# Gated delta rule: q's norm folded into the output's norm, with q's squares added on GpSimd

## The reference, cut to what is computed

```python
def l2norm(x):
    return x * rsqrt(sum(x * x, -1) + 1e-6)

q = l2norm(silu(conv(q_raw))) * 128 ** -0.5       # 8 heads of 128, each used by two value heads
k = l2norm(silu(conv(k_raw)))
# per value head (16) and direction (2), chunk by chunk:
#   qk = einsum(q, k) * decay
#   o_i = (q * exp(gc)) @ S + qk @ v_new
o = o_forward + flip(o_backward)
o = o * rsqrt(mean(o * o, -1) + 1e-6) * g_norm     # per token and head
y = (o * silu(z)) @ w_out
```

## Time and profile before

| | |
|---|---|
| median of 3 runs | 3367.14 us |
| lowest and highest | 3359.4 and 3367.23 us |
| span of the profiled execution | 3362.7 us |
| PE busy | 3184.5 us, 95% |
| DVE, ACT, POOL busy | 52%, 44%, 19% |
| granted TensorE clock, mean | 0.978 |

### The profile page before, as it was taken

How to read it: one execution, slowest core, us unless ns; L and a number is a source line. 1 busy time by engine, 2 the same in 40 slices (tenths; PEclk the granted TensorE clock), 3 DMA queues, 4 the chain that set the end, 5 groups by cost and what they waited for, 6 DMA issues and landing times. The chain is left out here.

```text
span 3362.7 us, 57300 instructions
## 1 busy us (share of the span) xinstructions
PE 3184.5 (95%) x22569; PEld 2066.8 (61%) x22569; DVE 1745.8 (52%) x3567; ACT 1475.9 (44%) x3027; POOL 637.6 (19%) x524
## 2 busy tenths in 40 slices
PE   5779999999999999999999999897999999999998
PEld 2347777777777764455445555444676767767663
DVE  1146666666666652244433334244666766666642
ACT  3135545545545531156423445234455555555521
POOL 0013322322232220011001010002323232232300
PEclk9789999999999999999999999897999999999999
DMA  9811111111111127022311012001112111111135
GB/s 376 305 40 39 41 45 34 50 41 45 50 41 45 31 65 261 0 61 67 123 32 38 25 39 88 32 16 50 36 43 55 42 54 38 54 40 42 42 109 193
DMA packets 216679, 238.16 MB, mean 71 GB/s; under 512 B 19290, under 2 KB 159780, under 8 KB 216292
## 3 DMA queue, kind: packets, MB, share of 16 engines
q1 hardware_dynamic: 216420, 234.57, 21.7%
HBM read 214.87 MB, written 19.66 MB: 70 GB/s over the span
## 5 line engine op out<-in xcount | busy, mean ns | idle before, releaser
L917 PE MATMUL ps<-hT,W 128*128 128x512 f32 (+1 forms) x2656 | 1007.9, 507 | 2.9 <-DVEq L192 2.0
L917 PEld LDWEIGHTS ps<-hT,W 128*128 128x128 f32 x2656 | 467.6, 192 | 206.0 <-issue 164.9
L1349 DVE CAST_PREDICATED arena<-mask,ps 128x384 bf16<-128x384 uint32 x448 | 252.5, 564 | 242.1 <-PE ps L986 180.0
L1168 ACT CAST arena<-ps 128x384 bf16<-128x384 f32 x384 | 166.5, 479 | 339.4 <-PE ps L973 339.0
L2352 PE MATMUL ps<-arena 128*128 128x512 f32 x712 | 311.1, 595 | 2.7 <-SPq L192 2.5
L1351 DVE CAST_PREDICATED arena<-mask,ps 128x384 bf16<-128x384 uint32 x448 | 249.9, 558 | 0.0
L2352 PEld LDWEIGHTS ps<-arena 128*128 128x128 f32 x712 | 134.6, 191 | 167.4 <-issue 162.6
L1987 PE MATMUL ps<-hT,W 128*128 128x512 f32 (+1 forms) x608 | 218.2, 493 | 0.9 <-DMA W<-in_att_w_in 0.7
L1461 POOL TENSOR_TENSOR arena<-arena 128x768 f32<-128x768 f32 (+1 forms) x32 | 43.5, 1360 | 921.2 <-ACT arena L1204 921.2
L1324 DVE SCALAR_TENSOR_TENSOR arena<-arena,vec 128x770 f32<-128x770 f32 (+1 forms) x192 | 189.6, 988 | 6.8
L986 PEld LDWEIGHTS ps<-arena 128*128 128x128 bf16 x2304 | 147.1, 99 | 50.8 <-issue 45.7
(11 more groups left out here) (290 smaller groups left out, 6105.9 us busy)
## 6 DMA issues: line engine op xcount, KB each, us to landing
arena<-in_ada_w SPq DMA_DIRECT2D x24, 2048.0 KB, 19.7
W<-in_gdn_w_in SPq DMA_DIRECT2D x95, 512.0 KB, 4.0
W<-decay_rows SPq DMA_DIRECT2D x64, 384.0 KB, 4.9
arena<-in_gdn_w_out SPq DMA_DIRECT2D x32, 512.0 KB, 10.3
W<-in_gdn_w_out SPq DMA_DIRECT2D x30, 512.0 KB, 3.4
arena<-gated SPq DMA_DIRECT2D x32, 384.0 KB, 8.2
gated<-arena SPq DMA_DIRECT2D x24, 384.0 KB, 2.4
W<-in_att_w_in SPq DMA_DIRECT2D x16, 512.0 KB, 4.0
```

The costliest lines, as they stand in the source:

```text
L917: mm = pe.matmul(ps[:, b, 0:t1 - t0], w[:, i, :], env.hT[:, i, t0:t1], start=(i == 0), stop=(i == KD - 1))
L1168: act.copy(half_cols(Xb[d], s, d), ps[:, 2 * d, 0:384].rearrange("p (c b s) -> p c b s", c=NT, s=s)).then_inc(*inxe.up(m, lv, d))
L1349: dve.copy_predicated(half_cols(Mb[d], s, d), wide(env.m4[:, d, lv]), src_m).then_inc(*inm.up(m, lv, d, "m"))
```

## The change

For q the sum by ones, Ln, Exp, the two table loads and DVE's product are taken out; G and the scan use q as SiLU leaves it. POOL forms q · (1e-6 · 128²) and multiplies that by q, into two new buffers `q2` (a q head serves two value heads, and the next q comes before the second is done). At the end of a slot POOL adds `q2` to the squares of o before PE may sum them. G and the decay rows no longer wait for `nrm` of q but for its SiLU. The new buffers move the tiles behind them by 6144 bytes per partition. Since the layer gets two more semaphores, some of the LRU's and the attention's are taken from this layer's names.

```diff
@@ fill_plan
-        normed = (["x1"] if short else ["x0", "x1"]) * (tile and n > -2)
+        normed = ["x0", "x1"] * (tile and n > -2 and n % 2 == 0)
@@ gdn_phase
-    v = carve(env, [..., ("sq", (T,)),
+    v = carve(env, [..., ("sq", (T,)), ("q2", (T,), 2),
...
-    xrs = seq("x_rs", [(n,) for n in TILES])
-    nrm = seq("nrm", [(n,) for n in TILES])
+    xrs = seq("x_rs", [(n,) for n in TILES if n % 2 == 0])
+    nrm = seq("nrm", [(n,) for n in TILES if n % 2 == 0])
...
+    qsc = seq("q_scaled", [(n,) for n in TILES if n % 2])
+    osf = seq("osf", [(m,) for m in U])
@@ tensor, fill
-                    if starts:
+                    if starts and n % 2 == 0:
                         pe.wait_ge(nrm.sem, nrm.at(n))
+                    elif starts:
+                        pe.wait_ge(sx.sem, sx.at(n, 1))
@@ scalar, keep
-                sc, e = (1.0 / P, 0) if use[0] == "o" else (1.0, 0) if n % 2 == 0 else (float(P), 1)
+                sc, e = (1.0 / P, 1) if use[0] == "o" else (1.0, 0)
@@ vector
-                if p == 14 and n in TILES:
-                    t = v.k if n % 2 == 0 else v.q
+                if p == 14 and n in TILES and n % 2 == 0:
                     dve.wait_ge(xrs.sem, xrs.at(n))
-                    lo = q_from(n)
-                    dve.tensor_tensor(t[:, lo:T], t[:, lo:T], v.sq[:, lo:T], ALU.mult).then_inc(*nrm.up(n))
+                    dve.tensor_tensor(v.k, v.k, v.sq, ALU.mult).then_inc(*nrm.up(n))
@@ gpsimd
             if n in TILES:
-                t = v.k if n % 2 == 0 else v.q
                 pool.wait_ge(sx.sem, sx.at(n, 1))
-                pool.wait_ge(og.sem, og.at(n - 1, 0))
                 lo = q_from(n)
-                pool.tensor_tensor(v.sq[:, lo:T], t[:, lo:T], t[:, lo:T], ALU.mult).then_inc(*sqx.up(n))
+                if n % 2 == 0:
+                    pool.wait_ge(og.sem, og.at(n - 1, 0))
+                    pool.tensor_tensor(v.sq, v.k, v.k, ALU.mult).then_inc(*sqx.up(n))
+                else:
+                    q2 = v.q2[(n + 1) // 2 % 2][:, lo:T]
+                    pool.tensor_scalar(q2, v.q[:, lo:T], EPS * P * P, None, ALU.mult).then_inc(*qsc.up(n))
+                    pool.wait_ge(qsc.sem, qsc.at(n))
+                    pool.tensor_tensor(q2, q2, v.q[:, lo:T], ALU.mult).then_inc(*sqx.up(n))
             if m in U:
-                pool.wait_ge(nrm.sem, nrm.at(n if n % 2 else n - 1))
+                pool.wait_ge(sx.sem, sx.at(n if n % 2 else n - 1, 1))
                 pool.wait_ge(eg.sem, eg.at(m, 1))
...
             if n in U:
                 pool.wait_ge(rue.sem, rue.at(n, NT - 1, 1, "o"))
-                pool.wait_ge(nrm.sem, nrm.at(n))
+                pool.wait_ge(nrm.sem, nrm.at(n // 2 * 2))
                 pool.wait_ge(og.sem, og.at(n - 1, 0))
                 ot = v.OT[:, n % 2, LO:T]
-                pool.tensor_tensor(v.sq[:, LO:T], ot, ot, ALU.mult).then_inc(*osq.up(n))
+                pool.tensor_tensor(v.sq[:, LO:T], ot, ot, ALU.mult).then_inc(*osf.up(n))
+                pool.wait_ge(osf.sem, osf.at(n))
+                pool.wait_ge(sqx.sem, sqx.at(n // 2 * 2 - 1))
+                pool.tensor_tensor(v.sq[:, LO:T], v.sq[:, LO:T], v.q2[n // 2 % 2][:, LO:T], ALU.add).then_inc(*osq.up(n))
@@ lru_phase (likewise wz, st, cv, og; in att_phase wkv, wq, st, ad, aev, szd)
-    wu = seq("w_u", per(*one), 16)
+    wu = Seq(env, "gdn_w_x", per(*one), 16)
```

More of the change, by code:

```diff
@@ L291, in vector @@
         dve.wait_ge(dve_s.sem, dve_s.next(0))
-        dve.memset(env.epsc[:, 1:2], EPS * P)
+        dve.memset(env.epsc[:, 1:2], EPS * EPS * P)
         dve.memset(env.epsc[:, 2:3], 0.0)
@@ L640, in gdn_phase @@
     NEG, KDEC, DCH = range(3)
-    v = carve(env, [("pad", (2, PADW)), ("acc", (2, CONVW)), ("q", (T,)), ("k", (T,)), ("kS", (T,)), ("sq", (T,)),
+    v = carve(env, [("pad", (2, PADW)), ("acc", (2, CONVW)), ("q", (T,)), ("k", (T,)), ("kS", (T,)), ("sq", (T,)), ("q2", (T,), 2),
                     ("vtok", (NT, P)), ("ktok", (NT, P)), ("sz", (2, T)), ("KK", (NT, P)), ("QK", (NT, P)),
@@ L1506, in lru_phase @@
     lama = Sig(env, "lru_lam_act", 1)
-    wu = seq("w_u", per(*one), 16)
-    wz = seq("w_z", per(*one), 16)
+    wu = Seq(env, "gdn_w_x", per(*one), 16)
+    wz = Seq(env, "gdn_w_z", per(*one), 16)
     wg = seq("w_g", per(*four), 16)
-    st = seq("st", per(*one), 16)
+    st = Seq(env, "gdn_st", per(*one), 16)
     ud = seq("u_done", per(*one))
@@ L1519, in lru_phase @@
     sq = seq("root", per(*two))
-    cv = seq("conv", per(*four))
+    cv = Seq(env, "gdn_convv", per(*four))
     iu = seq("iu", per(*[(d, i) for d in range(2) for i in range(2)]))
@@ L1523, in lru_phase @@
     scn = seq("scan", per((0,), (1,), (2,)))
-    og = seq("og", per(*two))
+    og = Seq(env, "gdn_og", per(*two))
     U0 = D
@@ L1846, in att_phase @@
     cst = seq("cst", [(k,) for k in ("band", "dup0", "dup1", "pdup0", "pdup1")])
-    wkv = seq("w_kv", [(g, i) for g in G for i in range(2)], 16)
-    wq = seq("w_q", [(g, u) for g in G for u in range(2)], 16)
+    wkv = Seq(env, "gdn_w_v", [(g, i) for g in G for i in range(2)], 16)
+    wq = Seq(env, "gdn_w_x", [(g, u) for g in G for u in range(2)], 16)
     wz = [seq("w_z", [(g,) for g in G], 16), Seq(env, "gdn_w_z", [(g,) for g in G], 16)]
-    st = seq("st", [(g,) for g in G], 16)
-    ad = seq("fill_done", order)
-    aev = seq("fill_act", [key for key in order if key[1] not in on_dve])
+    st = Seq(env, "gdn_st", [(g,) for g in G], 16)
+    ad = Seq(env, "gdn_fill_done", order)
+    aev = Seq(env, "gdn_fill_kept", [key for key in order if key[1] not in on_dve])
     dev = seq("fill_dve", [key for key in order if key[1] in on_dve])
@@ L1855, in att_phase @@
     rad = seq("rope", [(g, k) for g in G for k in ("k", 0, 1)])
-    szd = seq("silu_z", [(g,) for g in G])
+    szd = Seq(env, "lru_silu_z", [(g,) for g in G])
     sc = seq("scores", [(p, i) for p in PAIRS for i in range(2)])
```

## The result

The changed kernel takes 3374.02 us (median of 8 runs, 3369.39 to 3381.5), the kernel before, run beside it, 3360.81 (8 runs, 3356.78 to 3367.23). The ratio is 1.0033, with a 95% interval of 1.0023 to 1.0043: slower by 13.2 us by the medians, by 11 us by the ratio, and by 8 to 14 us by its interval. The forecast was 3369.6 us with a range of 3352 to 3379. The time lies in the range, but that is luck: the kernel before, 3367.14 us in the three runs shown then, came out 6.3 us lower in eight. Counted from its own base, the range allowed a rise of at most 11.9 us (3379 less 3367.14) and the forecast was a rise of 2.5. The medians rose by 13.2.

A forecast was written before the change was run, and what follows sets the result against it. PE was taken to bound the kernel, with waits behind DVE in layer 3's odd slots. Layer 0's -4.6 and layer 3's +7.1 us gave +2.5 on 3367.14, so 3369.6 us; range 3352 to 3379.

The forecast's parts named there:

- the small rows of the table: Start, slot 0 and even slots of the DeltaNet layers: forecast change 0.
- PE's sums in layer 0: Odd slots of layer 0: removing PE's sums over q saves 1.29 us each, -9.0 us over seven slots.
- x1: Layer 3, odd slots, position 12: removing this 512-column sum over q takes 0.86 us of PE's work but gains 0.
- The deal in layer 3: Odd slots of layer 3: redistributed filling matmuls leave positions 6 and 10 short, losing about 0.85 us per slot, +6.0 us.
- The wait at position 15: Layer 3, odd slots: PE's idle time before L996 grows from 0.85 to 1.7 us, with no gain.
- The ports and position 2 in layer 0: Odd slots of layer 0: POOL and DVE block each other, position 2 has less fill; L973 waits 0.4 us, +2.9 us.
- The walk through the lock: Start of layer 0's odd slots: POOL and DVE exclude each other, so masked copies start at 732.47 rather than 732.10.
- The slots 15: Slot 15 of each layer: PE waits for POOL's bare addition, +1.5 us in layer 0 and +1.1 in layer 3.
- Slot -1: Slot -1 of both layers: removed sums taken as 0, and POOL's new work ending before DVE's convolution, also 0.
- The price bounds: POOL's multiply by a constant, squaring q: between a one-input cast of 0.82 us and a two-input 1.47 us.
- The ports decide: Slower rival, chance 0.10: POOL's moved casts block DVE at all 28 slot boundaries, some 0.6 us each; +16.5 us, 3383.6.

The follow-up runs named there:

- the old deal: Changed kernel with filling matmuls dealt out as in the kernel before, the odd-slot sums over q counted but not issued; ratio to the kernel before 0.9999.
- the idle products: Changed kernel with POOL waiting for v's convolution in slot -1 and PE's removed products reissued there, result unused; ratio 1.0013, or 0.9976 issued twice with all repairs.

## Why the prediction was right and wrong

Of the rise that the forecast lacks (13.7 by the slots less 2.5, 11.2 us), slot -1 has 6.9, the odd slots of layer 0 have 3.9, slots 14 and 15 have 1.4 and the small rows of the table 1.0; layer 3 was forecast 2.0 too high. That the time fell into the range in spite of this is the luck of the base.

*PE's sums in layer 0: right.* 1.29 us per odd slot, measured 1.29; in layer 3 x1 is worth 0, as said.

*The deal in layer 3: right in mechanism, a third too large.* Forecast +0.85 per slot, measured +0.62, and the old deal gives exactly that back. The wait at position 15 grew to 1.2 us rather than 1.7, and the two waits of L973 came to 0.5 rather than 0.8.

*The ports and position 2 in layer 0: mechanism right, the term mis-sized.* "Together with position 2 ... L973 waits 0.4 us" was the step. Its 0.4 us measured 0.97. The walk through the lock put the masked copies 0.37 us late, and they came 0.54 late. It also took two costs of fill as just enough without the lock (0.4 us in all seven slots), where the deal alone costs 0.45 in each. Each size was small, but they add, and there are seven slots: -2.2 us instead of -6.1, the second largest part of the miss.

*The slots 15: size.* The addition was priced at the 1.47 and 1.04 of L1477. That line squares one tile. With two different tiles it takes 1.81 and 1.27, and the trace of before had that price in the products with the decay rows (count; busy us, mean ns; idle before):

```profile
L1467 POOL TENSOR_TENSOR W<-W,arena 128x768 f32<-128x768 f32 x32 | 57.4, 1814 | 115.9 <-DVE arena L1436 115.9
```

So L925 waited 2.57 and 1.61 us rather than the forecast 2.2 and 1.4:

```profile
1242.62 0.67 PE L925 MATMUL ps<-arena,cst 128*128 128x256 f32 x2 [2.57 <-POOL arena L1487]
...
3233.24 1.10 PE L925 MATMUL ps<-arena,cst 128*128 128x512 f32 x2 [1.61 <-POOL arena L1487]
```

Slot 14 of layer 0 added 0.8 us that I had not seen: L925 waits 2.5 us for ACT there rather than 1.7. I read it as L1338 late, then ACT's cast behind it, then the eviction that o1's bank needs; the run without the addition brings the 1.7 back.

*Slot -1: the step that failed.* "I take 0 there" stood for PE's sums, and "either way it ends long before DVE's next operation of two SBUF inputs in that slot, the convolution at 13" for POOL. The second holds in full slots, where 9.0 us lie between the end of SiLU (633.90) and the convolution (642.90) and POOL ends its four instructions at 641.5; in slot -1, without scan and fill, it is 3.2 us (249.47 to 252.64). I had noted that the slot is different and then priced POOL by the others, and I moved L1467 "from position 15 to 10" and said that it "wakes nobody earlier", without asking whom it would lie beside. The price bounds were wrong too: the multiply by a constant takes 2.13 us and the product behind it 1.81, above my 0.82 to 1.47. This gave 5.96 + 0.96 of the 11.2 us that were missing; 1.2 of them are the clock's, which the sums, priced at 0, had kept up.

*What the trace of before could have shown.* A cut of slot -1 (clock 0.89, PE busy for 36 of 48 us) would have said that PE's clock is at stake there, so that taking work from an idle PE is not free.

*The rivals.* "The ports decide" had its sign right. Its mechanism (DVE late at all 28 boundaries) didn't come: even slots stay within 0.05 us of their old length, slot 4 of layer 0 aside, and that one is as long in the run with nothing added to POOL.

## What to carry over

When an instruction's wait is loosened, list for every kind of stage, the first and the last among them, what it will now run beside; a POOL instruction off every path can still cost 4 us where it meets DVE's densest stretch. Where the code deals work out by shares, a removal moves everything else, so keep the old deal and take out only the step. And in a stage where PE is half idle, a product may be what keeps its clock up.

## What the hardware showed

- POOL, 768 columns of fp32: multiply by a constant 2.13 us (1.49 with 512), product or sum of two tiles 1.81 (1.27), square of one tile 1.47 (1.04), cast 0.82.
- A DVE operation with one tile as input (L1325, fp32 in SBUF) also got longer beside POOL: 0.61 us alone, 0.83 beside the decay-row products, 1.27 beside all of POOL's work. I had counted only those with two.
- PE's clock fell 1.3 us into a gap of 2.0 us in one kernel, and stayed through two gaps of 1.67 and 0.85 us in another (windows above).
- In slot -1 of layer 3 the clock returns 36.0 us into the slot in the kernel before (sums over q on PE, their logarithm on ScalarE), 35.3 to 36.3 in seven kernels with neither, and 29.4 with the idle products and no logarithm; with these the slot is 2.4 us shorter than before the change. Which difference from the kernel before does it was not looked into.
